# Modulation vectors: where twelve groups, four early groups of the next layer and the filter's sine features are computed

## The reference, cut to what matters

```python
sh1, sc1, g1, sh2, sc2, g2 = split(silu(c) @ ada_w + ada_b, 6)          # for the tokens
sh1c, sc1c, ...           = split(silu(c_ctx) @ ada_w + ada_b, 6)       # for the context
h = rmsnorm(x) * norm1_g * (1 + sc1) + sh1                              # needs sh1, sc1 alone
p = h @ w_in                                                            # the first projection
z = concat([t, cos(f w), -sin(f w)])                                    # positions, 1024 x 33
h = sin(fr1 * (z @ w1 + b1)); h = sin(fr2 * (h @ w2 + b2))              # the filter's features
x = x + g1 * mix;   h2 = modulate(rmsnorm(x), sh2, sc2);   x = x + g2 * experts(h2)
```

## Time and profile before

| | |
|---|---|
| time, median of 3 runs | 4172.25 us (4171.83 to 4175.88) |
| span of the profiled execution, first to last instruction | 4178.4 us |
| the profiled execution's own time | not listed apart from its span |
| mean granted TensorE clock | 0.958 of full speed |
| TensorE busy | 3794.1 us (91%) |
| VectorE, ScalarE, GpSimd busy | 2525.8, 1925.7, 778.6 us (60%, 46%, 19%) |
| `mods` | until 103.5, next stage from 107.0 us |
| `front1` | 107 to 509 us |
| start of `hgrn` | 971 us |

### The profile page before, as it was taken

The page is one execution under the profiler, slowest core; times in us unless marked ns, Lnnn a source line. Parts: engine busy times, 40 slices in busy tenths (PEclk is TensorE's granted clock), DMA queues, the critical chain, the costliest instruction groups (busy, mean ns, idle before and its releaser), DMA issues. The chain is left out here.

```text
span 4178.4 us, 44405 instructions
## 1 busy us (share of the span) xinstructions
PE 3794.1 (91%) x17525; PEld 2908.9 (70%) x17525; DVE 2525.8 (60%) x2685; ACT 1925.7 (46%) x2515; POOL 778.6 (19%) x565
## 2 busy tenths in 40 slices
PE   7999988897778889999999999799989898999988
PEld 2788744344677468877777788678877587787857
DVE  7421166444976778888888889652177535524753
ACT  4411110024647167777676767533166314424731
POOL 0200024220002111212111110420044223202422
PEclk9999989998898899999999999999999999999999
DMA  7323315113105689999999999434231343435123
GB/s 277 117 89 110 112 54 189 52 48 140 39 22 192 240 303 372 374 374 357 375 374 366 361 370 374 158 116 128 103 143 45 108 157 122 126 114 200 51 83 124
DMA packets 395169, 779.13 MB, mean 186 GB/s; under 512 B 26164, under 2 KB 109951, under 8 KB 394704
## 3 DMA queue, kind: packets, MB, share of 16 engines
q1 hardware_dynamic: 378706, 724.65, 48.5%
q0 software_dynamic: 11328, 41.16, 3.0%
q10 hardware_dynamic: 4928, 10.49, 0.7%
HBM read 664.73 MB, written 111.51 MB: 186 GB/s over the span
## 5 line engine op out<-in xcount | busy, mean ns | idle before, releaser
L2827 DVE TENSOR_TENSOR moe_w_low<-shared_z,moe_w_high 128x2048 fp32r<-128x2048 f32 x256 | 594.5, 2367 | 101.9 <-ACT moe_w_high L2780 101.1
L2780 ACT ACTIVATE moe_w_high<-shared_z 128x2048 fp32r<-128x2048 f32 x256 | 476.8, 1914 | 185.7 <-DMA shared_z<-in_exp_w 180.4
L172 PE MATMUL moe_bank<-moe_w_high,moe_xgT_high 128*128 128x512 f32 x1024 | 404.6, 395 | 20.1 <-DVE moe_w_low L2827 14.2
L174 PE MATMUL moe_bank<-moe_w_high,moe_xgT_low 128*128 128x512 f32 x1024 | 399.9, 391 | 0.0
L173 PE MATMUL moe_bank<-moe_w_low,moe_xgT_high 128*128 128x512 f32 x1024 | 399.6, 390 | 0.0
L2827 DVE TENSOR_TENSOR moe_w_low<-moe_w_raw,moe_w_high 128x2048 fp32r<-128x2048 f32 x128 | 287.4, 2286 | 64.4 <-ACT moe_w_high L2780 64.0
L2780 ACT ACTIVATE moe_w_high<-moe_w_raw 128x2048 fp32r<-128x2048 f32 x128 | 238.2, 1910 | 119.3 <-DMA moe_w_raw<-in_exp_w 118.1
L3053 POOL TENSOR_SCALAR layer_att_p<-layer_att_p,layer_att_rinv,layer_att_neg_lam 128x1280 f32<-128x1280 f32 (+1 forms) x72 | 173.2, 2405 | 530.1 <-DVE layer_att_neg_lam L3082 315.2
L3060 DVE TENSOR_REDUCE layer_att_nb<-layer_att_scores 128x1 f32<-128x1280 f32 (+1 forms) x144 | 195.0, 1369 | 89.5 <-PE layer_att_scores L2965 88.6
L172 PEld LDWEIGHTS moe_bank<-moe_w_high,moe_xgT_high 128*128 128x128 f32 x1024 | 192.9, 188 | 67.4 <-DVE moe_w_low L2827 17.1
L172 PE MATMUL layer_front_bank<-layer_front_w_high,layer_front_hT_high 128*128 128x512 f32 (+1 forms) x608 | 230.7, 379 | 7.6 <-POOL layer_front_hT_low L658 7.6
(11 more groups left out here) (543 smaller groups left out, 8801.8 us busy)
## 6 DMA issues: line engine op xcount, KB each, us to landing
shared_z<-in_exp_w SPq DMA_DIRECT2D x128, 2048.0 KB, 10.6
moe_w_raw<-in_exp_w SPq DMA_DIRECT2D x64, 2048.0 KB, 10.2
mods_raw<-in_ada_w SPq DMA_DIRECT2D x12, 2048.0 KB, 9.0
shared_z<-in_w_in SPq DMA_DIRECT2D x48, 512.0 KB, 6.5
first_raw<-in_w_in SPq DMA_DIRECT2D x32, 512.0 KB, 6.4
late_raw<-in_w_mod SPq DMA_DIRECT2D x8, 2048.0 KB, 7.9
proj_t<-front_out SPq DMA_DIRECT2D x48, 256.0 KB
shared_z<-in_w_out SPq DMA_DIRECT2D x12, 1024.0 KB, 6.2
```

Source lines behind the costliest of these rows:

```text
L172: nc.tensor.matmul(out, lhs[0], rhs[0], start=start, stop=False)
L174: return nc.tensor.matmul(out, lhs[1], rhs[0], start=False, stop=stop)
L2780: nc.scalar.activation(hi, x, ACT.Copy).then_inc(high, 1)
L2827: nc.vector.tensor_tensor(lo, x, hi.bitcast(F32), ALU.subtract).then_inc(low, 1)
```

## The change

- `mods` keeps groups 0 to 3. It has four buffers, so the four loads wait for nothing; the features, the stores of rows and the wait for them leave the stage. `ada_b` is also loaded as columns.
- `front1` takes groups 6 to 9 (as columns), 4, 5, 10 and 11 (as rows), and the four early groups of the next layers, in this order: 12 sums. GpSimd loads them, 1 MB at a time into four buffers, from i = 8 on. VectorE multiplies each 128 x 512 slice by its silu value per partition and adds it up (`Vectors.add`, two of eight slices in each job from i = 10; for the next layers' groups twice, for c and c_ctx). TensorE then sums over the partitions by a product with a column of ones (`Vectors.finish`), three jobs after the last slice.
- The features are computed there too (`Waves`), their layers after jobs 12 and 17.
- `hgrn` loses the late groups: loads, products, copies and stores.

```diff
          ("norm_g_2", 16), ("hy_norm_g", 4), ("hg_norm_g", 1), ("hy_conv_w", 36), ("hy_conv_b", 12)]
-VEC_B = [("hg_lb", 16), ("pool_scale_2", 4), ("subln_g_2", 2)]
+VEC_B = [("hg_lb", 16), ("pool_scale_2", 4), ("subln_g_2", 2), ("ada_b", 48)]
...
+    groups = [("ada_w", 0, g) for g in range(4)]
+    RING = len(groups)
+    RP = 2
     with Stage(core, "mods") as st:
...
-                    if i < len(groups):
-                        name, l, g = groups[i]
-                        if i >= RING:
-                            sp.wait_ge(low, 2 * (i - RING + 1) + 1)
-                        sp.dma_start(raw[i % RING][:, :, :],
-                                     io[name][l, :, g * BANK:(g + 1) * BANK].rearrange("(k p) n -> p k n", p=P)
-                                     ).then_inc(core.load[i % RING].sem, 16)
-                    if i == len(groups) - 1:
-                        ahead_w(sp)
-                    if 0 <= i - len(groups) < 2:
-                        sp.wait_ge(low, 2 * (i - 2) + 1)
-                        ahead_x(sp, i - len(groups))
-                    j = i - RING - 1
-                    if j >= 0:
-                        sp.wait_ge(bias_added, j + 1)
-                        sp.dma_start(core.mod_rows[0][:, j * BANK:(j + 1) * BANK], rows[j % RR][:, :]
-                                     ).then_inc(core.hstore[j % RR].sem, 16)
-                sp.wait_ge(sines, 2)
-                sp.dma_start(core.hy_wave, wave[:, :]).then_inc(waved, 16)
-                for j in range(RR):
-                    sp.wait_ge(core.hstore[j].sem, core.hstore[j].at(len(groups) // RR))
-                sp.wait_ge(waved, 16)
+                sp.dma_start(bias[:, :], io["ada_b"][0][0:nc_].partition_broadcast(2)).then_inc(biases, 16)
+                for i, (name, l, g) in enumerate(groups):
+                    sp.dma_start(raw[i][:, :, :],
+                                 io[name][l, :, g * BANK:(g + 1) * BANK].rearrange("(k p) n -> p k n", p=P)
+                                 ).then_inc(core.load[i].sem, 16)
+                ahead_w(sp)
+                for i in range(2):
...
-                    if layer:
-                        dve.wait_ge(sines, 1)
...
+
+class Vectors:
+
+
+    FIRST, STEPS, SLOTS, DONE = 10, 4, 4, 6
+    COLS, ROWS = (6, 7, 8, 9), (4, 5, 10, 11)
+
+    def __init__(self, core, st, whole, x, junk):
+        self.core, self.nc = core, core.nc
...
+        self.acc = [[t[:, v * BANK:(v + 1) * BANK] for v in range(2)] for t in whole]
+        self.rows = [junk[0:2, r * BANK:(r + 1) * BANK] for r in range(2)]
...
+
+    def fill_pick(self, pool):
+        self.core.pool(pool, self.nc.gpsimd.memset(self.pick[:, :], 1.0))
+        self.nc.gpsimd.memset(self.pick[:, 1:3], 0.0).then_inc(self.picks, 1)
+
+    def load(self, pool, h):
+        j, half = divmod(h, 2)
+        if h >= self.SLOTS:
+            jj, used = divmod(h - self.SLOTS, 2)
+            pool.wait_ge(self.summed if used else self.half_used, jj + 1)
+        kind, g = self.jobs[j]
+        k = half * (KD // 2)
+        src = (late_weights(self.core, g, k, k + KD // 2) if kind == "late" else
+               self.core.io["ada_w"][0, k * P:(k + KD // 2) * P, g * BANK:(g + 1) * BANK].rearrange("(k p) n -> p k n", p=P))
+        pool.dma_start(self.raw[h % self.SLOTS][:, :, :], src).then_inc(self.loaded[h % self.SLOTS], 16)
+
...
+
+        j, c = divmod(q, self.STEPS)
+        kind, _ = self.jobs[j]
+        h = 2 * j + c // 2
+        if c == 0 and j >= 2:
+            dve.wait_ge(self.finished, j - 1)
+        if c % 2 == 0:
+            dve.wait_ge(self.loaded[h % self.SLOTS], 16 * (h // self.SLOTS + 1))
+        sides = (16, 24) if kind == "late" else (0,)
+        for k in range(2 * c, 2 * c + 2):
+            w = self.raw[h % self.SLOTS][:, k % (KD // 2), :]
+            for v, at in enumerate(sides):
+                acc, f = self.acc[j % 2][v], self.core.silu[:, at + k:at + k + 1]
+                if k == 0:
+                    ins = self.nc.vector.tensor_scalar(acc, w, f, None, ALU.mult)
+                else:
+                    ins = self.nc.vector.scalar_tensor_tensor(acc, w, f, acc, ALU.mult, ALU.add)
+            if k == KD // 2 - 1:
+                ins.then_inc(self.half_used, 1)
+                dve.wait_ge(self.half_used, j + 1)
+            elif k == KD - 1:
+                ins.then_inc(self.summed, 1)
+            else:
+                self.core.dve(dve, ins)
+
+    def finish(self, pe, j):
+        kind, _ = self.jobs[j]
...
+        a = self.acc[j % 2]
+        if j == 0:
+            pe.wait_ge(self.picks, 1)
+        pe.wait_ge(self.summed, j + 1)
+        if 2 <= r < 2 + self.NR:
+            pe.wait_ge(self.biased, r - 1)
+        elif r >= 2:
+            pe.wait_ge(self.copied, r - 1 - self.NR)
+        if kind == "col":
+            for s in range(4):
+                o = 2 * (4 * j + s)
+                last = self.nc.tensor.matmul(self.col_bank[:, o:o + 2], a[0][:, s * P:(s + 1) * P], self.pick[:, 3:5],
+                                             start=True, stop=True)
+        elif kind == "row":
+            last = self.nc.tensor.matmul(self.row_bank[r % 2][0:2, :], self.pick[:, 3:5], a[0], start=True, stop=True)
+        else:
+            self.nc.tensor.matmul(self.row_bank[r % 2][0:2, :], self.pick[:, 0:2], a[0], start=True, stop=False)
+            last = self.nc.tensor.matmul(self.row_bank[r % 2][0:2, :], self.pick[:, 2:4], a[1], start=False, stop=True)
+        last.then_inc(self.finished, 1)
+
...
+        core, c0 = self.core, 4 * self.COLS[0]
+        dve.wait_ge(self.finished, self.NC)
+        b = core.col_b[:, AT_B["ada_b"] + c0:AT_B["ada_b"] + c0 + 16]
+        core.dve(dve, self.nc.vector.tensor_tensor(core.mod1[:, c0:c0 + 16, :],
+                                                   self.col_bank[:, 0:32].rearrange("p (c v) -> p c v", v=2),
+                                                   b.unsqueeze(2).to_broadcast([P, 16, 2]), ALU.add))
+        core.dve(dve, self.nc.vector.scalar_tensor_tensor(core.sc[2][:, :], core.mod1[:, 32:40, 0], 1.0,
+                                                          core.col_a[:, AT_A["norm2_g"]:AT_A["norm2_g"] + 8], ALU.add, ALU.mult))
+
...
+        r = j - self.NC
+        dve.wait_ge(self.finished, j + 1)
+        if r == 0:
+            dve.wait_ge(self.biases, 32)
+        self.reuse_row(dve, r)
+        self.nc.vector.tensor_tensor(self.rows[r % 2], self.row_bank[r % 2][0:2, :], self.bias[r], ALU.add).then_inc(self.biased, 1)
+
+    def copy(self, act, j):
+        r = j - self.NC
+        act.wait_ge(self.finished, j + 1)
+        self.reuse_row(act, r)
+        self.nc.scalar.activation(self.rows[r % 2], self.row_bank[r % 2][0:2, :], ACT.Copy).then_inc(self.copied, 1)
...
+    def store(self, sp, j):
+        r = j - self.NC
+        kind, g = self.jobs[j]
+        if kind == "row":
+            sp.wait_ge(self.biased, r + 1)
+            to = self.core.mod_rows[0][:, g * BANK:(g + 1) * BANK]
+        else:
+            sp.wait_ge(self.copied, r - self.NR + 1)
+            to = late_rows(self.core, g)
+        sp.dma_start(to, self.rows[r % 2]).then_inc(self.kept[r % 2].sem, 16)
...
+class Waves:
+
+
+    LOAD, LAYER, BEND, WRAP, SINE, KEEP = 10, (12, 17), (13, 18), (14, 19), (15, 20), 22
...
+    def load(self, sp):
+        io = self.core.io
+        sp.dma_start(self.pos, io["t_pos"]).then_inc(self.position, 16)
+        sp.dma_start(self.w1[:, :], io["hy_pos_w1"][0]).then_inc(self.position, 16)
+        sp.dma_start(self.w2[:, :], io["hy_pos_w2"][0]).then_inc(self.position, 16)
+
+    def layer(self, pe, n):
+        w_, x = ((self.w1, self.pos), (self.w2, self.wave))[n]
+        if n:
+            pe.wait_ge(self.sines, 1)
+        else:
+            pe.wait_ge(self.position, 48)
+        for t in range(2):
+            last = self.nc.tensor.matmul(self.bank[t][0:HFF, :], w_[:, :], x[:, t * BANK:(t + 1) * BANK], start=True, stop=True)
+        last.then_inc(self.layer_done, 1)
...
+    def sine(self, act, n):
+        act.wait_ge(self.bounded, n + 1)
+        self.nc.scalar.activation(self.wave, self.lin, ACT.Sin).then_inc(self.sines, 1)
+
+    def keep(self, sp):
+        sp.wait_ge(self.sines, 2)
+        sp.dma_start(self.core.hy_wave, self.wave).then_inc(self.kept, 16)
...
                         sp.wait_ge(low, KD * G)
                         sp.wait_ge(turned, 2 * n)
+                        if vectors:
+                            sums.wait_stores(sp)
+                            sp.wait_ge(waves.kept, 16)
                         filter_inputs(sp)
...
+                    if vectors:
+                        if i == Waves.LOAD:
+                            sp.wait_ge(turned, 2 * n)
+                            waves.load(sp)
+                        if i == Waves.KEEP:
+                            waves.keep(sp)
+                            sums.load_biases(sp)
+                        for j in range(sums.NC, sums.N):
```

(61 more changed lines are left out.)

161 lines of the change are left out of this document (80 added, 81 removed).

## The result

The changed kernel takes **4114.24 us** (4111.13 to 4123.09, 4 runs) against 4172.04 us (4164.69 to 4175.88, 4 runs) of the kernel before: ratio 0.9862, 95% interval 0.985 to 0.9873. The forecast was 4116.0. In a later comparison on another occasion the same kernel had 4116.99 (4115.03 to 4118.69) against 4173.51, ratio 0.9865 (0.9848 to 0.9881).

The account below looks back on a forecast made before the run. TensorE, busy 91% of the span, was taken as the bound, alone in the first projection. First stage -58.0, first projection +20.3 and recurrence -18.5 sum to -56.2, taking 4172.25 to 4116.0 us; range 4104 to 4138.

Parts of the forecast that it names:

- First stage, -58.0: `mods`: fewer groups, no features and no store at the end let the next stage start at 48.95 instead of 106.99 us.
- First projection, +20.3: `front1`: TensorE has no idle time, so added rows, late groups, columns, features and breaks are all paid; bounds 18.9 and 26.
- the breaks: `front1`: 14 insertions each break TensorE's stream by some 0.1 us, 1.4 us in all.
- Recurrence, -18.5: Start of `hgrn`: v and masks land earlier, first score product at 997 to 999 instead of 1018.56; bounds 0 and 24.
- the chain of VectorE: Start of `hgrn`: after its exponents, VectorE's updates and level products set the pace, from about 986 to 996.6 us.
- the first scores at 26 to 28 us: `hgrn`: first score product expected at 997 to 999 us; listed sign: 27 to 28 us into the stage instead of 47.5.
- 1.5 that I took off for the low clock: Start of `hgrn`: the recurrence's gain of 20 us reduced by 1.5 for products at TensorE's low clock.
- the gates' early start: `hgrn`: ScalarE's gates of the next head, formerly behind the late rows, start together with the rest of the recurrence; unpriced.
- The rest, 0: Stages between and behind the changed ones: they keep their work and only start earlier, change 0.
- Nothing back in the recurrence: Rival, `hgrn`: late products ran beside other work and low clock stretches first scores, so no gain; 4134.5 us, chance 0.12.
- VectorE late at the changes of group: Rival, `front1`: VectorE's sums delay the weight split, seven times 2.8 us; 4135.6 us, chance 0.12.
- GpSimd's queue starving VectorE: Rival, `front1`: slices load too slowly, VectorE and then TensorE stop, 113 us lost; 4229 us, chance 0.04.

Follow-up runs that it names:

- experiment 3: Changed kernel plus one 256 KB store, and SyncE's wait for it, at the end of the first stage; 4116.04 us, ratio 0.9868.
- experiment 2: Changed kernel with the four late groups' sums computed nowhere, their rows filled from the bias; 4112.42 us, ratio 0.986.
- experiment 5: Changed kernel with VectorE's sums and GpSimd's loads in the first projection at twice the pace, two slices in a job; 4115.83 us, ratio 0.9868.
- experiment 6: Changed kernel with 32 unused identity products on TensorE between the first turn and its wait for v in `hgrn`; 4105.57 us, ratio 0.9843.
- experiment 1: Changed kernel with the four late groups moved back from `front1` to the start of `hgrn`; 4134.12 us, ratio 0.9911.
- experiment 11: Changed kernel with first weight load first, first head's v first, and 14 filler products ahead of `hgrn`'s first turn; 4114.94 us, ratio 0.985.

## Why the prediction was right, point by point

**First stage, -58.0: right at each mark.** Forecast and measured: first product 21.05 and 20.35, turn of the fourth group 46.5 and 46.16, last vector 48.4 and 48.03, next stage 48.95 and 48.54. The only mark off by more than 0.41 is the first. The large loads were hidden as said; the store at the end was worth 3.0 of it (3.48 to 0.51), and experiment 3 brings 2.2 of that back. That the other 55 or so are the eight groups and the features rests on these marks, which follow from what a group costs; no run puts a group or the features back.

**First projection, +20.3: right in sum, by two errors that cancel.** With the costs read around the insertions, four sets of columns cost 3.6, four rows 4.6, four late groups 8.0 and two layers 4.1: 20.4, and 424.53 - 403.95 is 20.6. I had 4.2, 3.6, 7.2 and 3.9, and 1.4 for the breaks. Columns were cheaper than their nearest row (four with their break 0.91, where the row has 1.06 for four without), while a break around products with 512 moving columns costs 0.2 to 0.25 rather than 0.1. The multiply-adds take 0.75, not 0.69, which nothing pays. That they are hidden at all is shown by experiments 2 and 5. Of the four costs only that of the late groups was also measured by a run (8.1, experiment 2); the others are read from the insertions of one trace. That the sum came out as forecast is thus in part luck.

**Recurrence, -18.5: right in mechanism, too small by 6.4 us.** Data at 12.4 us into the stage (12.05 measured), first update at 14.9 (14.9), updates and level products 10.6 (10.3): the chain of VectorE was right, and the first score product came 22.2 us earlier where the steps gave 20. The 6.4 are three amounts: 2.2, for I put the first scores at 26 to 28 us where the chain's own steps made 25.5; 1.5 that I took off for the low clock on top of that chain (it does cost 1.3 ahead of the scores by experiment 6, but from the data's arrival to the first update there are 2.85 us with it, where I had 2.5 without); and 2.7 gained behind the first scores, which no step contained. The low clock is in these 2.7 with its price: the first 14 score products took 3.36 where experiment 1 had 1.73. The groups of VectorE's scan from the first scores on, in the kernel before, the changed kernel and experiment 1, show where the gain lies:

```profile
L2040 DVE TENSOR_TENSOR_SCAN hyena_forward<-hyena_forward 128x1280 f32<-128x1280 f32 x6 | 16.9, 2817 | 4.4 <-ACT hyena_forward L1820 4.4
```

```profile
L2179 DVE TENSOR_TENSOR_SCAN hyena_forward<-hyena_forward 128x1280 f32<-128x1280 f32 x6 | 16.9, 2816 | 0.5 <-ACT hyena_forward L1978 0.5
```

```profile
L2219 DVE TENSOR_TENSOR_SCAN hyena_forward<-hyena_forward 128x1280 f32<-128x1280 f32 x6 | 16.9, 2817 | 4.5 <-ACT hyena_forward L1999 4.5
```

VectorE's 4.4 us of idle time before this group, ended by ScalarE, have become 0.5. ScalarE began the next head's gates 47.3 us into the stage before, behind the late rows' copies, almost together with the scores; now it begins at 18.3, ahead of them (954.57 in the timeline above). The line of the kernel before:

```profile
1018.38 1.28 ACT L1805 ACT_TABLE_LOAD   x1
```

Less 1.6 for the scores at the low clock, the 3.9 saved are 2.3 of the 2.7. Experiment 1 agrees: with the late groups back, the idle time is 4.5 again and the part behind the first scores takes 233.1 again. The prediction named the gates' early start and gave it no price.

**The rest, 0: +2.5 in `filter` and `hyena`, and the scatter of the experts.** `filter` took 168.8 to 172.1 and `hyena` 289.7 to 293.5 over all variants, none of which touches them, so no cause inside the change is shown. What the first stage, the first projection and the recurrence sum to (-62.1) and what the medians differ by (-57.8) are 4.3 apart. The forecast of 4116.0 is so close by luck: the recurrence's extra gain and this remainder nearly cancel. How much of the remainder the change causes stays open.

**The rivals.** Nothing back in the recurrence: refuted, experiment 1 turns 23.6 us on and off. VectorE late at the changes of group: refuted, TensorE is 100% busy there and stays so at twice the pace. GpSimd's queue starving VectorE: refuted likewise; loads land in 5.9 us, where one per 10.9 is asked for. The Trainium skill ("SBUF — State Buffer", the trap of DVE and SWDGE under "two separate sides") has GpSimd's loads wait while VectorE runs an instruction of its two-port mode. No run here shows such a wait holding VectorE up, not even with VectorE at 90% in experiment 5; whether the later landings there (8.3 and 6.3 us) are this, or two loads under way at once beside the stage's others, no run separates. The low clock at the start of `hgrn` is real, and worth 1.3 us before the scores while the data come last, and 1.6 in them. The Trainium skill ("TensorE: Matmul & The Clock Gate", Part 1) has the array fall back when idle, and the trace agrees: in experiment 6 the granted clock is still 1.00 behind the wait of 2.01 us, and 0.51 from 955 us on, behind the wait of 1.55 and in that of 2.69. That the late products had brought the clock back in the kernel before is not in the prediction's row; the trace has 0.50 in 953 to 980 us and 1.00 in 980 to 993.

## What to carry to other kernels

Where TensorE is full, move small matrix-vector work to an engine with room and leave TensorE one closing product per sum; price each insertion by the starts around it, not by the product's duration. Work used to fill an early wait has to be checked for what it holds back on every queue: here it delayed the data by some 10 us, the first states by 14, the first scores by 22 and ScalarE's next gates by 29. Before filling an idle TensorE to keep its clock up, find whose chain ends last; where that was another engine, as in experiment 11, the higher clock bought nothing.

## What the runs showed of the hardware

- A multiply-add of 128 x 512 with a scalar per partition takes 749 ns, and the plain multiply of the same shape 478.
- A product with 512 moving columns takes 0.90 us in a row of its own kind; set into the dense stream here it delayed it by 1.15, and two together by 2.01.
- The pace of TensorE at the start of the first stage rose at moments that differ between executions: the stage scattered by 1.4 us (47.20 to 48.60), with 14 to 19 products between 24 and 28 us.
- Loads of 1 MB on GpSimd's queue landed in 5.9 and 5.7 us (medians) at one per 10.9 us, and in 8.3 and 6.3 at twice that pace beside a VectorE at 90%.
- A stage bound by loads from memory varied by 14 us (1143 to 1157) between executions of nearly the same program, more than most changes tried here are worth.
